# GLU groups of a decoder trunk: three 256-column products a weight tile, or one of 512 and one of 256 columns

## What is computed

```python
def conv_recurrent_mixer(hn, w_in, ...):
    u = hn @ w_in                                   # 2048 -> 4096 columns
    a_val, a_gate, xr, gr = jnp.split(u, [D_A, 2 * D_A, 2 * D_A + D_B], axis=-1)
    ya = a_val * jax.nn.sigmoid(a_gate)             # the GLU, 1024 channels
    ya = causal_depthwise_conv(ya, conv_a_w, conv_a_b)          # 31 taps
    ya = jax.nn.silu(layer_norm(ya, ln_a_g, ln_a_b))
    xr = causal_depthwise_conv(xr, conv_b_w, conv_b_b)          # 4 taps
    yb = rg_lru(xr, ...) * jax.nn.gelu(gr)
    return jnp.concatenate([ya, yb], axis=-1) @ w_out
```

## Time and profile before

| | |
|---|---|
| median of 3 runs | 2327.21 us |
| the profiled execution | 2326.66 us |
| its span, first to last instruction | 2324.9 us |
| granted clock of TensorE, mean | 0.998 |
| PE busy | 2303.3 us (99%) |
| DVE busy | 1511.6 us (65%) |
| ACT busy | 1225.7 us (53%) |
| POOL busy | 82.0 us (4%) |
| chain that ended last | PE 87%, DVE 8%, ACT 2%, DMA 2% |

### The profile page before, as it was taken

How to read it: one execution, slowest core, us unless ns; L and a number is a source line. 1 busy time by engine, 2 the same in 40 slices (tenths; PEclk the granted TensorE clock), 3 DMA queues, 4 the chain that set the end, 5 groups by cost and what they waited for, 6 DMA issues and landing times.

```text
span 2324.9 us, 36441 instructions
## 1 busy us (share of the span) xinstructions
PE 2303.3 (99%) x12830; PEld 2016.2 (87%) x12830; DVE 1511.6 (65%) x1802; ACT 1225.7 (53%) x1524; POOL 82.0 (4%) x99
## 2 busy tenths in 40 slices
PE   8999999999999999999999999999999999999997
PEld 7899998888888888888888888888888888888887
DVE  8899876556556555678767666666456556555676
ACT  7875754445445435456666566554345345345454
POOL 0048000000000000000000000000000000000000
PEclk9999999999999999999999999999999999999999
DMA  8563765655655655655555555556656655655643
GB/s 256 183 188 122 226 183 193 209 175 189 208 181 181 210 187 181 200 188 174 181 179 168 172 168 171 182 181 207 191 181 199 195 184 193 194 185 195 190 152 120
DMA packets 366809, 431.40 MB, mean 186 GB/s; under 512 B 13312, under 2 KB 299136, under 8 KB 366720
## 3 DMA queue, kind: packets, MB, share of 16 engines
q1 hardware_dynamic: 366432, 429.97, 58.4%
q10 hardware_dynamic: 288, 0.23, 0.0%
HBM read 428.05 MB, written 2.10 MB: 185 GB/s over the span
## 4 chain that ended last, share of the span: by engine, by line
PE 87%; DVE 8%; ACT 2%; DMA 2%; issue 1%; SPq 0%; DVEq 0%; ACTq 0%
PE ps L513 32%; PE ps L710 30%; PE ps L519 16%; DVE Z L1870 3%; PE ps L511 2%; DVE spl L1404 2%; PE ps L518 1%; DMA raw<-in_w_in 1%; PE ps L556 1%; PE ps L557 1%; PE ps L558 1%; ACT spl L928 1%; PE O L691 0%; DVE pp L1682 0%; PE Z L665 0%
## 5 line engine op out<-in xcount | busy, mean ns | idle before, releaser
L1404 DVE TENSOR_TENSOR spl<-raw,spl 128x1024 fp32r<-128x1024 f32 x793 | 951.1, 1229 | 573.0 <-ACT spl L928 567.8
L928 ACT ACTIVATE spl<-raw 128x1024 fp32r<-128x1024 f32 (+1 forms) x801 | 822.2, 1055 | 681.9 <-PE ps L710 342.3
L513 PE MATMUL ps<-XA,spl 128*128 128x512 f32 x1792 | 455.8, 393 | 7.9 <-DVE spl L1642 7.0
L513 PE MATMUL ps<-XB,spl 128*128 128x512 f32 x1760 | 462.8, 393 | 0.0
L513 PEld LDWEIGHTS ps<-XA,spl 128*128 128x128 f32 x1792 | 318.9, 189 | 59.4 <-issue 7.8
L710 PE MATMUL ps<-spl,XA 128*128 128x512 f32 x1536 | 349.7, 389 | 0.0
L710 PE MATMUL ps<-spl,XB 128*128 128x512 f32 x1536 | 349.7, 389 | 0.0
L513 PEld LDWEIGHTS ps<-XB,spl 128*128 128x128 f32 x1760 | 305.8, 188 | 42.4
L710 PEld LDWEIGHTS ps<-spl,XA 128*128 128x128 f32 x1536 | 287.8, 188 | 59.5
L710 PEld LDWEIGHTS ps<-spl,XB 128*128 128x128 f32 x1536 | 287.8, 188 | 59.5
L519 PEld LDWEIGHTS ps<-XB,spl 128*128 128x128 f32 x1760 | 259.2, 190 | 31.1
(11 more groups left out here) (210 smaller groups left out, 1735.3 us busy)
## 6 DMA issues: line engine op xcount, KB each, us to landing
raw<-in_w_up SPq DMA_DIRECT2D x256, 512.0 KB, 4.1
raw<-in_w_down SPq DMA_DIRECT2D x256, 512.0 KB, 4.9
raw<-in_w_qkv SPq DMA_DIRECT2D x96, 512.0 KB, 4.5
raw<-in_w_gate SPq DMA_DIRECT2D x64, 512.0 KB, 4.5
raw<-in_w_in SPq DMA_DIRECT2D x63, 512.0 KB, 4.8
raw<-in_w_out SPq DMA_DIRECT2D x32, 512.0 KB, 4.5
raw<-in_w_o SPq DMA_DIRECT2D x32, 512.0 KB, 4.6
raw<-in_w_proj SPq DMA_DIRECT2D x8, 512.0 KB, 5.2
```

Source lines behind the costliest of these rows:

```text
L513: pe.matmul(ps[:, b + o, :], w[:, q, 0, c], x[:, kt, :, :], start=start, stop=False)
L928: return act.activation(out, in_, ACT.Copy, scale=scale)
L1404: dve.tensor_tensor(s[:, :, 1, :], raw[:, m % NRAW, :, :], s[:, :, 0, :].bitcast(F32), ALU.subtract).then_inc(lo_ready, 1)
```

## The change

The GLU groups go from small_gemm to gemm: one product of 512 and one of 256 columns a tile, two banks a group. ACT copies the cross half of each group, DVE adds it to the first half and keeps the sum in PSUM (the tile O, bank 1), then a second instruction scales it by rB. The counts of copies and the waits of the PSUM ring are set to that: whole_weights, which goes back to one bank a group, gets the first waits that small_gemm had. In ACT's list the sigmoid of gate 0 moves behind splits 6 and 7 and is preceded by the gate's copy; the copy of value 0 stands behind split 0, that of a later value c at q == 4, behind split 4 of the pair before (behind 14 products where that pair has no splits left).

```diff
         def crossed(g):
-            return g - sum(n for first, n in ((G_MLP0, 32), (G_GATE0, 32), (G_OUT1, 8), (G_GATE1, 32)) if g >= first)
+            return g - sum(n for first, n in ((G_MLP0, 24), (G_GATE0, 32), (G_OUT1, 8), (G_GATE1, 32)) if g >= first)
...
             def small_gemm(g, m, x, tiles, rows, mid=None):
-                pe.wait_ge(sum_ready, g - 1 if g == G_GLU else g - 2 if g - G_GLU < 3 else g - 3)
+                pe.wait_ge(sum_ready, g - 3)
...
             def whole_weights(g, m, x):
-                pe.wait_ge(sum_ready, g - 3)
+                pe.wait_ge(sum_ready, g - 1 if g == G_OUTB else g - 2 if g - G_OUTB < 3 else g - 3)
...
-            small_gemm(G_GLU, C_GLU, XA, None, rows)
-            small_gemm(G_GLU + 1, C_GLU + 4, XA, None, rows)
-            for g in range(2, 8):
-                small_gemm(G_GLU + g, C_GLU + 4 * g, XA, None, rows)
+            for g in range(8):
+                gemm(G_GLU + g, 0, C_GLU + 4 * g, 0, XA)
@@ ScalarE's list @@
             def glu_gate(c):
-                act.wait_ge(sum_ready, G_GLU + 2 * c + 2)
+                take_cross(G_GLU + 2 * c + 1, 0, (chunk_used, C_GLU + 8 * c + 8))
+                act.wait_ge(glu_gated, c + 1)
                 act.activation(tv[:, :, :], tv[:, :, :], ACT.Sigmoid).then_inc(glu_sig, 1)
...
             split(C_GLU + NSPL)
+            take_cross(G_GLU, 0, (chunk_used, C_GLU + 4))
             rg_sqrt(1)
...
             split(C_GLU + NSPL + 5)
-            glu_gate(0)
             split(C_GLU + NSPL + 6)
             split(C_GLU + NSPL + 7)
+            glu_gate(0)
...
                     if c < 3:
                         split(C_GLU + NSPL + 8 * c + q)
+                    if q == 4:
+                        take_cross(G_GLU + 2 * c, 0, (chunk_used, C_GLU + 8 * c + 4))
@@ VectorE's list @@
-            def take_scaled(g, m, out):
-                dve.wait_ge(chunk_used, m + 4)
-                dve.tensor_tensor(out, ps[:, g % 4, :].rearrange("p (o n) -> p o n", o=2), bcast(rB[:, :], 2),
-                                  ALU.mult).then_inc(sum_ready, 1)
+            def take_scaled(g, out):
+                total = O[:, 1, :].rearrange("p (o n) -> p o n", o=2)
+                take_sum(g, 0, total)
                 dve.wait_ge(sum_ready, g + 1)
+                return dve.tensor_tensor(out, total, bcast(rB[:, :], 2), ALU.mult)
...
             def glu_gate(c, meanwhile=None):
-                take_scaled(G_GLU + 2 * c + 1, C_GLU + 8 * c + 4, tv[:, :, :])
+                take_scaled(G_GLU + 2 * c + 1, tv[:, :, :]).then_inc(glu_gated, 1)
                 if meanwhile is not None:
                     meanwhile()
+                dve.wait_ge(glu_scaled, c + 1)
                 dve.wait_ge(glu_sig, c + 1)
```

More of the change, by code:

```diff
@@ L243, in trunk @@
         glu_sig = sem("glu_sig")
+        glu_scaled = sem("glu_scaled")
+        glu_gated = sem("glu_gated")
         glu_ready = sem("glu_ready")
@@ L1815, in _ @@
             rg_scan(0)
-            def take_scaled(g, m, out):
-                dve.wait_ge(chunk_used, m + 4)
-                dve.tensor_tensor(out, ps[:, g % 4, :].rearrange("p (o n) -> p o n", o=2), bcast(rB[:, :], 2),
-                                  ALU.mult).then_inc(sum_ready, 1)
+            def take_scaled(g, out):
+                total = O[:, 1, :].rearrange("p (o n) -> p o n", o=2)
+                take_sum(g, 0, total)
                 dve.wait_ge(sum_ready, g + 1)
+                return dve.tensor_tensor(out, total, bcast(rB[:, :], 2), ALU.mult)
             def glu_value(c):
-                take_scaled(G_GLU + 2 * c, C_GLU + 8 * c, glu[:, 2 * c:2 * c + 2, PAD_A:])
+                take_scaled(G_GLU + 2 * c, glu[:, 2 * c:2 * c + 2, PAD_A:]).then_inc(glu_scaled, 1)
             def glu_gate(c, meanwhile=None):
-                take_scaled(G_GLU + 2 * c + 1, C_GLU + 8 * c + 4, tv[:, :, :])
+                take_scaled(G_GLU + 2 * c + 1, tv[:, :, :]).then_inc(glu_gated, 1)
                 if meanwhile is not None:
                     meanwhile()
+                dve.wait_ge(glu_scaled, c + 1)
                 dve.wait_ge(glu_sig, c + 1)
```

## The result

The changed kernel takes 2336.53 us (median of 6 runs, 2335.33 to 2337.90) against 2327.13 us for the kernel before (6 runs, 2326.23 to 2327.95): 9.4 us more, ratio 1.004, 95% interval 1.003 to 1.005. The forecast was 2339.4, in a range of 2332.0 to 2345.5; the measured time lies in that range, but 2 us under the bounds of 2338.5 to 2340.9 that the forecast gave its own mechanism. The profiled execution took 2336.43 us, 9.77 more than that of before.

What follows compares the result with a forecast made beforehand. DVE was taken to bound the GLU stage. Sums 4.8, value 0 2.8, gate 0 5.3, idle times -1.15, value 1 0.3 and value 3 0.2 gave 12.2 us: 2327.2 to 2339.4 us, range 2332.0 to 2345.5.

Steps and rivals of the forecast that it cites:

- The bound: GLU stage: DVE sets the end, so its delay reaches the end one for one; time saved on PE becomes wait.
- The products: PE in the GLU groups: 256 pairs save 2.3 us on a waiting engine, worth 0, at most 2.3.
- Value 0: First value sum on DVE: it waits 2.8 us for ACT's copy, which stands behind two splits.
- Gate 0: First gate sum on DVE: it waits 5.3 us (4.4 to 5.8) for ACT's copy behind split 7 and its load.
- Value 1: Second value sum on DVE: ACT's copy behind split 4 and later loads cost about 0.3 us.
- Value 3: Last value sum on DVE: ACT's copy comes after 10 products, a wait of 0.2 us.
- The sums: Eight added DVE sums in the GLU groups, 0.60 us each: 4.8 us (5.8 at most), all on the path.
- rival B: DVE's splits collide with GpSimd, so the cost exceeds the sum: 18.1 us, 2345.3 us; chance 0.14.
- rival A: The added work comes but ACT reaches its copies in time, so no waits: 4.8 us, 2332.0 us; chance 0.15.
- The ring: Two PSUM slots of two banks delay PE's group starts, but cost nothing beyond DVE's lag.
- C: PE's clock falls after idling at five group starts: 7.7 us if none were hidden, 2347.1 us; chance 0.06.
- D: PE is the bound and DVE's added work fits beside it: -2.3 us, 2324.9 us, or no change; chance 0.05.

Runs made afterwards that it cites:

- narrow_before: The kernel before with GpSimd's low parts and most sums of taps cut to a few columns: 2325.18 us against 2326.88 for the kernel before.
- products_alone: The kernel before with only the new products and two-slot PSUM ring, no copies or sums, cross product left out: 2327.33 us against 2327.46 for the kernel before.
- gate_early: The changed kernel with ScalarE's copy and sigmoid of gate 0 moved back before splits 6 and 7: 2332.37 us against 2327.46 for the kernel before.
- value_early: The changed kernel with ScalarE's copy of value 0 moved ahead of the tanh of the recurrence's second half: 2333.25 us against 2327.46 for the kernel before.
- no_sum: The changed kernel without DVE's eight sums, still waiting for each copy, cross product left out: 2334.33 us against 2326.88 for the kernel before.
- sums_twice: The changed kernel with each of DVE's eight sums made twice, the second waiting for the first: 2340.01 us against 2327.46 for the kernel before.
- narrow_after: The changed kernel with GpSimd's low parts and most sums of taps cut to a few columns: 2332.93 us against 2326.88 for the kernel before.

## Why the prediction was right, and where its sizes were off

- **The bound.** "A delay of DVE in this stretch goes to the end one for one": 9.31 us of lag, 9.4 us of time, and over the experiments that add or remove waits and work on DVE the two agree to within 1.3 us. Where DVE got faster than PE (narrow_before), the time followed by 1.7 of 6.69 us only; the sentence holds for delays.
- **The products: worth 0, at most 2.3 us.** Right by products_alone (-0.1).
- **The waits.** Value 0: 2.61 us for 2.8. Gate 0: 4.98 for 5.3; the load behind split 7 took 4.5 us instead of 4.8. Value 1: for 0.3 us 0.56 in front of a split (153.47) and 0.1 at the sum (158.24). Value 3: 0.2 as said (an instruction that needn't wait starts 0.1 us before the end of the one ahead, 206.96). The three idle times of 1.15 us went as said. gate_early and value_early show that these waits are in the time, products_alone that the ring by itself is not.
- **The sums.** 8 x 0.61 us of pitch for 8 x 0.60. Their size on DVE was right, but not all of it arrives at the end, as the next point shows.
- **The mis-sized term.** The sum of 12.2 us had no term for collisions; they stood in rival B alone, where more work was to meet more of them ("two more", +4.4 us, beside "could remove or add such"). They have the other sign: three instructions beside GpSimd got shorter by 0.74, 0.70 and 1.36 us and one split longer by 0.11 (1.68 to 1.79), 2.7 us together. With it the sum is 9.5, and 9.4 was measured. Without such a term the time fell below the forecast's own bounds and into the wider range only because that reached down to rival A, for another reason. The smaller cost is not luck of one timing in its direction, as no_sum and sums_twice move the same way; its size depends on when DVE and GpSimd meet. The Trainium skill ("SBUF — State Buffer", section "Who interferes with whom") says that a DVE instruction with two SBUF inputs contends with a GpSimd instruction that reads SBUF, by an exclusive lock, and one with at most one SBUF input, outside its two-port modes, does not. The trace agrees: the instructions that got long, splits and multiplications, read two SBUF tiles (1.23 to 3.40 us), while the convolution steps, which read one tile from SBUF and one from PSUM, keep their length (mean 482 and 479 ns in the two kernels, 482 and 481 ns with GpSimd narrowed).
- **The ring.** Groups 4 and 5 start at 158.99 and 172.59 (158 and 172.5 said), the first whole-weights product at 207.81 (208.4 said). The sign "waiting 2 to 4 us at the starts of groups 3 to 5" came for group 4 alone: the waits were 0.30, 3.84 and 0.63 us. Behind the late split, which held PE up in group 1 and not in group 2 as said, and again in group 4, products ran at half pace for a while, so that PE came later to groups 3 and 5 by itself.
- **Rivals.** A (the waits don't come) falls with the two waits. C happened on PE and is hidden, as its "against" said: the granted clock is 0.71 and 0.68 in two stretches, and the group after each still waits for DVE (0.30 us at 143.72, 0.63 us at 172.59). D falls: PE has waits of 9 us and the time is longer. The Trainium skill ("TensorE: Matmul & The Clock Gate", section "HAM oscillation — how this bites in real kernels") says that gaps between bursts of products can drop the clock again and again. The trace agrees for these two gaps, but in gate_early three gaps of 2.31, 2.35 and 2.22 us left it at 1.00. In this kernel the fall cost no time that could be measured.

## What to carry to other kernels

Fewer columns on an engine that waits are worth nothing; what an extra step costs is read from the order in which the engine that must do it first does its other work: here a copy of 0.58 us stood behind a split whose load had not landed, and DVE waited 4.98 us for it; with the copy ahead of that split it waited 1.31. An instruction that is long only beside another engine, as DVE's were beside GpSimd here, can hold a wait: then work put ahead of it is partly free, work taken away is partly not gained, and a sum of durations that keeps such rows constant comes out too high.

## What was not expected of the hardware

In the kernel before products ran at half pace only at the start, after 7.0 us without work, and the granted clock fell once more, to 0.50, only among the last few products, behind 2313 us. In the changed kernel products slowed in mid-stage. After 2.31 us of wait PE began again at 127.65, and from about 129.1 us on rounds of four products took 1.28 us instead of 0.70, about the ratio of the two levels of 2.4 and 1.2 GHz; from 132.81 on they took 0.70 again (0.71 granted on average from 127 to 132 us). The same followed the wait of 3.84 us (0.68 from 160 to 165 us), while after waits of 0.30, 0.63 and 0.96 us at other group starts the clock stayed at 1.00. The length of the wait alone does not decide it: in gate_early the same wait of 2.31 us at the same place, 127.65, left the clock at 1.00, and so did one of 3.04 us in sums_twice (128.23), whereas in narrow_after one of 1.79 us (128.56) was followed by 0.66 from 128 to 133 us. What does decide it is open.

DVE's long instructions are long by GpSimd's work: with GpSimd narrowed, no split takes over 1.23 us and the multiplication of gate 3 takes 0.68 or 0.69 us, so what such rows have above 1.23 and 0.68 us is the wait for GpSimd.
